# Router logits of a hybrid encoder layer: router weights stationary in four column quarters, rows moving, and a summing product

## The reference

```python
h2  = rms_norm(x, ffn_norm_g)                      # x after the mixer, 1024 x 1024
gl  = h2 @ w_group  + b_group                      # 1024 x 4
el  = h2 @ w_expert + b_expert                     # 1024 x 16
# top-1 of 4 groups by gl, top-2 of its 4 experts by el, softmax weights
```

## Time and profile before

| what | value |
|---|---|
| median of 3 runs | 1025.11 us (1024.98 to 1025.66) |
| profiled execution, its time | 1026.02 us |
| its span | 1024.2 us |
| PE busy | 959.2 us (94%), 7896 instructions |
| PE weight loads busy | 756.8 us (74%) |
| DVE busy | 590.7 us (58%) |
| ACT busy | 208.8 us (20%) |
| POOL busy | 158.7 us (15%) |
| DMA | 109.71 MB |
| mean granted PE clock | 0.973 |

### The profile page before, as it was taken

The page is one execution under the profiler, slowest core; times in us unless marked ns, Lnnn a source line. Parts: engine busy times, 40 slices in busy tenths (PEclk is TensorE's granted clock), DMA queues, the critical chain, the costliest instruction groups (busy, mean ns, idle before and its releaser), DMA issues.

```text
span 1024.2 us, 19170 instructions
## 1 busy us (share of the span) xinstructions
PE 959.2 (94%) x7896; PEld 756.8 (74%) x7896; DVE 590.7 (58%) x1771; ACT 208.8 (20%) x494; POOL 158.7 (15%) x244
## 2 busy tenths in 40 slices
PE   5989999999999999999999996987899999999993
PEld 5687777687696697787878765565887887878872
DVE  2356875785775776675677468588324434444242
ACT  1233233331341332323323223110000000000000
POOL 7010010010010001001001003000323323334221
PEclk9999999999999999999999996997899999999997
DMA  9900101001000010010100119014457877879210
GB/s 318 351 21 2 43 1 43 22 22 42 21 23 21 22 42 22 22 43 1 43 22 1 42 32 359 15 49 165 123 193 278 304 249 262 298 267 326 89 59 28
DMA packets 48529, 109.71 MB, mean 107 GB/s; under 512 B 10288, under 2 KB 11568, under 8 KB 48432
## 3 DMA queue, kind: packets, MB, share of 16 engines
q1 hardware_dynamic: 32880, 82.87, 22.6%
q0 software_dynamic: 13824, 25.20, 7.2%
q10 hardware_dynamic: 1728, 0.26, 0.1%
HBM read 108.30 MB, written 25.17 MB: 130 GB/s over the span
## 4 chain that ended last, share of the span: by engine, by line
PE 88%; DVE 8%; issue 2%; ACT 1%; DMA 0%; DVEq 0%; ACTq 0%; POOL 0%; POOLq 0%
PE pm L352 83%; PE pm L355 5%; DVE X L1294 1%; DVE Y L1492 0%; DVE w_sb L986 0%; DVE X L1490 0%; DVE xt L1502 0%; DMA xt<-in_x 0%; DVE pqkv L1154 0%; DVE bs L1352 0%; DVE hT L1112 0%; DVE pqkv L1502 0%; DVE bs L977 0%; DVE bs L978 0%; DVE bs L976 0%
## 5 line engine op out<-in xcount | busy, mean ns | idle before, releaser
L352 PEld LDWEIGHTS pm<-hT,w_sb 128*128 128x128 f32 x1544 | 175.8, 193 | 6.3 <-DVE hT L1112 3.4
L352 PE MATMUL pm<-hT,w_sb 128*128 128x128 f32 x1544 | 176.9, 277 | 2.8 <-DVE hT L1112 2.8
L352 PE MATMUL pm<-w_sb,hT 128*128 128x512 f32 (+1 forms) x384 | 145.3, 529 | 0.0
L352 PE MATMUL pm<-wo_sb,pT 128*128 128x512 f32 x256 | 114.6, 599 | 1.4 <-ACT pT L847 0.7
L352 PEld LDWEIGHTS pm<-w_sb,hT 128*128 128x128 f32 x384 | 70.6, 190 | 56.2 <-issue 51.2
L1154 DVE SCALAR_TENSOR_TENSOR pqkv<-ci,cw,pqkv 128x128 f32<-128x128 f32 x288 | 77.7, 347 | 19.0 <-ACT pqkv L786 18.6
L352 PE MATMUL pm<-ctmp,w_sb 128*128 128x128 f32 x768 | 88.4, 276 | 0.1
L352 PEld LDWEIGHTS pm<-wo_sb,pT 128*128 128x128 f32 x256 | 47.6, 192 | 55.1 <-issue 53.2
L352 PEld LDWEIGHTS pm<-ctmp,w_sb 128*128 128x128 f32 x768 | 86.8, 192 | 0.3 <-issue 0.3
L1584 POOL TENSOR_TENSOR tail<-tail,rows 128x512 f32<-128x512 f32 x8 | 10.2, 1270 | 465.1 <-ACT aTm L805 465.1
L352 PE MATMUL pm<-w_sb,Y 128*128 128x512 f32 x152 | 68.7, 595 | 4.1 <-DVE Y L1492 4.1
(11 more groups left out here) (288 smaller groups left out, 1489.4 us busy)
## 6 DMA issues: line engine op xcount, KB each, us to landing
w_sb<-in_w_gate_up SPq DMA_DIRECT2D x12, 2048.0 KB
w_sb<-in_w_down SPq DMA_DIRECT2D x12, 1024.0 KB
w_sb<-in_w_in SPq DMA_DIRECT2D x5, 2048.0 KB, 17.2
wo_sb<-in_w_gate_up SPq DMA_DIRECT2D x4, 2048.0 KB
xt<-in_x SPq DMA_DIRECT2D x8, 512.0 KB, 3.5
wo_sb<-in_w_out SPq DMA_DIRECT2D x1, 4096.0 KB, 22.2
sc<-in_x SPq DMA_DIRECT2D x8, 512.0 KB, 3.4
out<-sc SPq DMA_DIRECT2D x8, 512.0 KB, 2.8
```

The source lines that it names most:

```text
L352: return pe.matmul(o_, lhsT=l_, rhs=r_, start=start, stop=stop, skip_group_check=True)
```

## The change

The router's weights are padded from 20 to 32 columns per `k` (`QUARTER` = 32) and become the stationary operand, `hT2[:, k, :]` the moving one with 128 columns. Product `k` writes partitions 32 (k mod 4) to 32 (k mod 4) + 31 of the first late bank, so `k` and `k + 4` accumulate in one quarter. That leaves four partial sums of 20 logits by 128 rows, one under the other. ACT copies these 128 x 128 values to `lg_sums`. A second product has `lg_sums` as stationary and `pick_sums` (a 32 x 20 identity four times over) as moving operand; it adds the four and turns them into 128 rows x 20, in columns 128 to 147 of the same bank. In the interior bodies this `sum_logits` stands on PE at level 1, ACT's copy behind its Y copy of level 0, and DVE's `copy_logits` moves from level 0 to level 1. In tile 7's body the sum stands at level 5 and ACT's copy at level 4. POOL makes `pick_sums` with four small copies at the start.

```diff
-        w_rt = sb("w_rt", [KD, NL])
+        w_rt = sb("w_rt", [KD, QUARTER])
+        pick_sums, lg_sums = sb("pick_sums", [NL]), sb("lg_sums", [P])
 ...
-                    ins = mm(late_banks(t)[0][:, 0:NL], hT2[:, k, :], w_rt[:, k, :], k == 0, k == KD - 1)
-                ins.then_inc(B.logits_done, 1)
+                    q = k % 4 * QUARTER
+                    ins = mm(late_banks(t)[0][q:q + QUARTER, 0:P], w_rt[:, k, :], hT2[:, k, :], k < 4, k > 3)
+                ins.then_inc(B.quarters_done, 1)
+
+            def sum_logits(t):
+                pe.wait_ge(B.quarters_ready, t + 1)
+                mm(late_banks(t)[0][:, P:P + NL], lg_sums[:, :], pick_sums[:, :]).then_inc(B.logits_done, 1)
 ...
                 logits(t)
+                sum_logits(t)
                 rows_ahead()
 ...
+                    if l == 1 and nx is not None and pv is not None:
+                        sum_logits(pv)
                     if nx is None:
+                        if l == 5:
+                            sum_logits(pv)
 ...
+            def copy_quarters(t):
+                act.wait_ge(B.quarters_done, t + 1)
+                act.activation(lg_sums[:, :], late_banks(t)[0][:, 0:P], ACT.Copy).then_inc(B.quarters_ready, 1)
 ...
                 square_xm(t)
+                copy_quarters(t)
 ...
+                    if pv is not None and l == (0 if nx is not None else 4):
+                        copy_quarters(pv)
 ...
-                    v.scalar_tensor_tensor(lg[:, self.t, :], late_banks(self.t)[0][:, 0:NL], bs[:, 89:90], b_rt,
+                    v.scalar_tensor_tensor(lg[:, self.t, :], late_banks(self.t)[0][:, P:P + NL], bs[:, 89:90], b_rt,
 ...
+                    if l == 1 and pv and nx:
+                        pv.copy_logits()
                     if l == 0:
-                        if pv and nx:
-                            pv.copy_logits()
-
 ...
+            for q in range(0, P, QUARTER):
+                step(g.tensor_copy(pick_sums[q:q + QUARTER, :], ident[q:q + QUARTER, q:q + NL]))
```

More of the change, by code:

```diff
@@ L49 @@
 TOPK = 2
+QUARTER = P // 4
 RANKS = T // P
@@ L229, in build @@
                  " top_found sc_ready p_ready p_turned pT_ready pv_done sink_in sink_exp yb_ready y_turned yT_ready out_done"
-                 " xm_ready ss2_ready hm_ready hm_turned hT2_ready logits_done lg_ready back_step late_step")
+                 " xm_ready ss2_ready hm_ready hm_turned hT2_ready quarters_done quarters_ready logits_done lg_ready back_step late_step")
         R = sems("iotas route_step exp_in exp_out picks counts totals hots gate_hots rows_summed gates_summed rows_ready"
@@ L1696, in laid_out @@
     routes = np.concatenate([np.asarray(inputs["w_group"]), np.asarray(inputs["w_expert"])], axis=2)
-    by_row["w_router"] = routes.reshape(KD, P, NL).transpose(1, 0, 2)
+    by_row["w_router"] = np.pad(routes.reshape(KD, P, NL).transpose(1, 0, 2), ((0, 0), (0, 0), (0, QUARTER - NL)))
     return {**inputs, **by_row}
```

## The result

The changed kernel takes 1029.07 us (median of 6 runs, 1028.32 to 1030.11) against 1025.05 us before. The ratio is 1.0043 with a 95% interval of 1.0031 to 1.0055. I had forecast 1024.7 us with a range of 1022.6 to 1028.0: wrong, and outside the range. The profiled execution took 1028.64 us with a span of 1026.8 us. It lies only 2.6 us above that of before, because the profile of before has 321.3 us behind its last lg instruction (1024.2 - 702.94), where all other profiles of this study have 319 to 320. It alone has 3.4 us at half speed from 1006.2 us on, in the experts (0.66 of the clock from 1005 to 1010 us). So the two traces are compared stage by stage, and the verdict is taken from the runs.

The account below looks back on a forecast made before the run. DVE's queue was taken to bound the six interior tiles, PE to be late in tile 7's body. Terms +0.5 (interior), -1.0 (tile 7's body), +0.1 (load) gave -0.4 on 1025.11: 1024.7 us, range 1022.6 to 1028.0.

Parts of the forecast that it names:

- What bounds the interior: Six interior bodies: DVE's queue reaches the X update nearly with PE, so PE's saving gains 0.27 us, not 1.2.
- The quarters: PE's logits in four column quarters: 0.45 us plus 0.1 for the shape change, instead of 1.79 us.
- The rival of serial quarters: Quarters don't run side by side, each record keeps 0.11 us: 1027.8 us; chance 7%.
- The sum: PE's extra product behind the X products in each interior tile: +0.14 us, bounds 0.03 to 0.32.
- The wait for lg: Interior: PE's turns of qkn wait for the moved DVE lg instruction, 0.21 us after the old start.
- my bound of 0.32: Upper bound on an interior tile's net effect: sum at its dearest and a wait of 0.27 us.
- the 0.15 that I allowed the period: Sign to check: the period of an interior tile stays 82.3 us within 0.15.
- Tile 7's body: Router's tile 6, where PE is late before X: earlier logits give -1.0 us, bounds 0 to -1.18.
- What could be late next: Tile 7's body: ACT's Exp, behind the new copy, ends about 670.9, before PE's turns of the scores need it.
- The rival of the clock: PE's new 0.9 us interior waits lower its clock, up to 1.65 us a tile: 1026.3 to 1034 us; chance 10%.
- The last tile: Quarters, copy and sum in series finish before DVE's reciprocal root, slack at least 0.4 us: costs nothing.
- POOL's copies: Start: four more small copies before masks_made, covered by the 5.87 us that ACT's chunk 1 copy waited for PE.

Follow-up runs that it names:

- e6: Changed kernel with DVE's scaling of y_mix moved behind level 0's XT update in the interior bodies: period 81.84 us, 1025.01 us, ratio 0.9998.
- e7: Kernel before with DVE's scaling of y_mix moved behind level 0's XT update: period 82.37 us, 1025.37 us, ratio 0.9999.
- e12: Changed kernel with the eight quarter products made twice over in the six interior bodies: period 82.50 us, 1028.49 us, ratio 1.0037.
- e5: Changed kernel with PE's sum ahead of level 1's products and DVE's lg instruction ahead of its z wait, interior bodies: period 82.01 us, 1025.08 us, ratio 0.9998.
- e2: Changed kernel with the new logits in tiles 6 and 7 alone, the interior as before: 1025.82 us, ratio 1.0014.
- e3: Changed kernel plus eight needless 128 x 128 products on PE in tile 7's body: 1025.11 us, ratio 1.0009.
- e11: Changed kernel with sum early, lg early and y_mix scaling late in the interior, plus eight needless products in tile 7's body: 1018.96 us, ratio 0.9944.
- e8: Changed kernel with three interior moves (sum early, lg early, y_mix scaling late): period 81.37 us, 1021.71 us, ratio 0.9960.
- e9: Changed kernel unaltered, measured once more for spread and a second profile: 1028.77 us, ratio 1.0044.
- e1: Changed kernel with the change in the six interior bodies alone, logits of tiles 6 and 7 as before: 1027.23 us, ratio 1.0024.

## Why the prediction was wrong

*What bounds the interior: right.* I said that DVE's queue would take the saving down to 0.27 us. X gained 0.28 (167.10 to 171.28 is 4.18 us, 166.43 to 170.89 was 4.46). e6, e7 and e12 show it from three sides.

*The quarters: right.* The step from the logits to the next products is 0.57 us, forecast 0.55. The records start in groups of four, and eight of them after the second half of hT2 take 0.35 us up to the next shape (670.83 to 671.18). The rival of serial quarters is out.

*The sum: mis-sized.* +0.14 forecast, +0.22 measured. The sum took its whole 2 x 0.11 us on top of the way from the X products to the projection: 172.60 - 171.74 = 0.86 us, before 171.98 - 171.36 = 0.62. I had let it take over part of the projection's entry. *The wait for lg: mis-sized.* +0.21 forecast against the old start. From level 2's first products to the turns it was 177.42 - 176.81 = 0.61 us, now 178.29 - 177.42 = 0.87, so +0.26. e5 takes both terms away and the period falls by their sum. Together the net of a tile is -0.28 + 0.22 + 0.26 = +0.20 us instead of +0.08: 1.2 us in all, 0.7 more than forecast. It lies within my bound of 0.32, but outside the 0.15 that I allowed the period.

*Tile 7's body: the step that failed.* The term was -1.0 us and held nothing for the clock. The gain itself came: X was 0.96 us earlier (671.97 against 671.05 in a body that began 1.88 us later), and DVE carried that to V. But in "What could be late next" I asked only which instruction would be late, and found ACT's Exp in time. I did not ask how long PE would then wait, and at what clock it would come out of the wait. From X to the kd_vt products it is 6.85 us before (671.05 to 677.90) and 6.84 us after (671.97 to 678.81), so the time won at X moves both engines alike and lengthens no wait. What changed is PE's own work in between. It ended 6.33 us behind X before (676.23 + 1.15), with the half-speed stretch from 671.7 to 675.1 us in it, and 4.96 us behind X after (675.78 + 1.15), with no such stretch. Those 1.37 us are the growth of the wait. Behind the wait of 1.87 us PE was granted 1.2 GHz for 10.2 us, across an output projection that nothing hides: 28.91 us from lg to lg instead of 25.17, 3.7 us lost for 1.0 won. The term measured about +2.8 us instead of -1.0.

*The rival of the clock* had the right mechanism in the wrong place. I put it at the new waits of 0.9 us in the interior, where dense projections stand around each wait; PEclk stays at 9 there, in e12 too, where the same place holds more PE work. For tile 7 I wrote that the mechanism might spare half-speed stretches, "worth a microsecond at most since DVE leads there". It did spare the one at 671.7 to 675.1 us, where DVE led and nothing was to be gained. The longer wait that this left was followed by one where PE leads.

*The last tile and POOL's copies: right.* PE got the sum done at 706.6 with lg written at 707.59; chunk 1's copy still waited 5.52 us for PE at the start. The 0.67 us by which the tiles begin later are PE's clock, which rose to full at 17.8 us of this trace and at 16.4 of the other. That moment lies anywhere between 16.1 and 19.0 in the profiles of this study, and the tiles follow it without the change too: with the interior as before, tile 0's lg instruction starts at 171.90, 172.36 and 173.18 us where the clock rose at 16.4, 17.3 (e2) and 18.9 (e7). So it is not the change's.

Two slips in the prediction's arithmetic change nothing: 4% and 5% are 9% and were entered as 0.10, and the clock's price in six tiles comes to 1034.6 us, not 1034.

The account: +1.2 (interior, shown by e5 and the periods) - 1.0 (X in tile 7) + 3.7 (clock) = +3.9 us, measured +4.0. The terms come from single profiles and the +4.0 from medians that scatter by 1 to 2 us, so an agreement within 0.1 us is in part luck. That PE's work in the wait removes the loss is shown (e3, e11 against e8). That the length of PE's wait alone decides is not: the same 1.87 us had 3.4 us at half speed behind it in three kernels (e2, e5, e6) and 10.2 in three others (after, e8, e12), and what selects between them stays open. It may go by the execution and not by the kernel, since the three with 3.4 us were profiled in executions at or near their fastest; but e9, with 10.2, was profiled in its fastest as well. How the form of tile 6's logits decides on the stretch ahead of the wait is not shown either, only that it did in all 14 profiles. And 1 us of e1's median stays open: its profile shows two more stretches in an execution of 1030.2 us, and none of the others was profiled.

## What to carry to other kernels

Before crediting a shorter product, find the instruction that the engine waits for next, and read the other engine's queue up to it: here 1.2 us of PE saving was worth 0.28 us, and moving one 0.75 us DVE instruction was worth another 0.66. Place a new step in the wait that the change itself opens (the sum ahead of X, lg ahead of z), not behind it. And where an engine gets through a sparse stretch faster, for fewer steps or for a better clock, ask how long it then waits and what its clock will be in the dense stretch that follows, since that may cost more than the step gained.

## What the runs showed that I had not expected

Needless PE work can pay: 16 records of 128 x 128 in a wait of 1.87 us made the changed kernel 3.7 us faster (1028.77 to 1025.11) and the best one 2.8 us (1021.71 to 1018.96), and did nothing where PE's wait had been 0.52 us. The sizes come from medians taken at different times, of e8 and e11 on different chips; the ratios to the kernel before are 1.0044 to 1.0009, and 0.9960 to 0.9944, the latter two with intervals that overlap.

Four column quarters of full height run four abreast in float32 with 128 moving columns: 16 records in 0.57 us with the change of shape, 32 in 1.01 us, so 0.44 us for 16 more, 0.028 us each. Full-width records took 0.11 us each with 20 moving columns, and with 128 moving columns 16 of them took 677.76 - 675.82 = 1.94 us in e3, 0.12 each. What a quarter record would take alone no run shows, so the factor is against full-width records. The Trainium skill (TensorE: Matmul & The Clock Gate, Part 3) reports 2.38 times for three column tiles; this trace has 0.11 / 0.028, about four times for four.
